# Seven-product sigmoid-gate projections, with sums of the normalised input made early and weight sums made by VectorE

## The reference

```python
h = rmsnorm(x, norm_g)
proj = einsum('bsd,dc->bsc', h, w_in)
a_qkv, z_a, b_qkv, z_b, r_a, r_b = split(proj, ...)   # r_a, r_b: 1024 columns each
y_a = einsum('bsc,cd->bsd', attn_a * silu(z_a), w_pa)  # K = 256
y_b = einsum('bsc,cd->bsd', attn_b * silu(z_b), w_pb)  # K = 512
merged = sigmoid(r_a + b_merge[:1024]) * y_a + sigmoid(r_b + b_merge[1024:]) * y_b
out = rmsnorm(x + einsum('bsd,de->bse', merged, w_out), final_g)
```

## Time and profile before

| | us |
|---|---|
| median of 3 runs | 443.84 (443.66 to 444.29) |
| the profiled execution, its time | 443.48 |
| the profiled execution, its span | 441.7 |
| PE busy | 431.6 |
| DVE, ACT, POOL busy | 212.8, 198.5, 176.3 |

### The profile page before, as it was taken

The page is one execution under the profiler, slowest core; times in us unless marked ns, Lnnn a source line. Parts: engine busy times, 40 slices in busy tenths (PEclk is TensorE's granted clock), DMA queues, the critical chain, the costliest instruction groups (busy, mean ns, idle before and its releaser), DMA issues.

```text
span 441.7 us, 6258 instructions
## 1 busy us (share of the span) xinstructions
PE 431.6 (98%) x2377; PEld 374.5 (85%) x2377; DVE 212.8 (48%) x367; ACT 198.5 (45%) x401; POOL 176.3 (40%) x113
## 2 busy tenths in 40 slices
PE   7899999999999999999999999999999999999995
PEld 6789998899889988988888888888888888888885
DVE  3831244344435446757857664827025173083334
ACT  5743555335544464567555554533223543332111
POOL 4744442243243333646499543534355354200000
PEclk9999999999999999999999999999999999999999
DMA  8962234622452263024122022222222284210421
GB/s 284 286 192 96 96 96 83 159 96 95 91 150 97 96 168 110 25 96 143 49 95 96 0 73 96 96 72 96 95 71 96 95 261 156 113 66 0 149 90 47
DMA packets 40044, 48.31 MB, mean 109 GB/s; under 512 B 3768, under 2 KB 35536, under 8 KB 40016
## 3 DMA queue, kind: packets, MB, share of 16 engines
q1 hardware_dynamic: 37568, 47.72, 34.4%
q10 hardware_dynamic: 2448, 0.21, 0.4%
HBM read 39.48 MB, written 2.15 MB: 94 GB/s over the span
## 4 chain that ended last, share of the span: by engine, by line
PE 96%; DMA 2%; DVE 1%; ACT 1%; SPq 0%; issue 0%; DVEq 0%; ACTq 0%
PE ps L766 20%; PE ps L770 20%; PE ps L767 20%; PE ps L816 4%; PE ps L818 4%; PE ps L817 4%; PE ps L890 3%; PE ps L974 3%; PE ps L975 3%; PE ps L973 3%; PE ps L873 3%; PE ps L917 3%; PE ps L907 2%; DMA xs<-in_x 2%; PE ps L865 1%; PE ps L850 0%
## 5 line engine op out<-in xcount | busy, mean ns | idle before, releaser
L662 POOL TENSOR_TENSOR w_lo<-raw,w_hi 128x1024 fp32r<-128x1024 f32 (+1 forms) x59 | 138.1, 2342 | 175.4 <-ACT w_hi L990 175.4
L766 PE MATMUL ps<-hT_hi,w_hi 128*128 128x512 f32 x336 | 135.0, 402 | 1.1 <-DVE hT_lo L1241 1.1
L770 PE MATMUL ps<-hT_lo,w_hi 128*128 128x512 f32 x336 | 131.2, 390 | 0.0
L767 PE MATMUL ps<-hT_hi,w_lo 128*128 128x512 f32 x336 | 131.1, 390 | 0.0
L770 PEld LDWEIGHTS ps<-hT_lo,w_hi 128*128 128x128 f32 x336 | 63.1, 188 | 13.5
L766 PEld LDWEIGHTS ps<-hT_hi,w_hi 128*128 128x128 f32 x336 | 63.2, 188 | 11.2 <-issue 1.3
L767 PEld LDWEIGHTS ps<-hT_hi,w_lo 128*128 128x128 f32 x336 | 63.3, 188 | 9.9
L990 ACT CAST w_hi<-raw 128x1024 fp32r<-128x1024 f32 (+1 forms) x58 | 59.2, 1020 | 8.3 <-PE ps L770 5.4
L816 PE MATMUL ps<-w_hi,hT_hi 128*128 128x256 f32 x160 | 45.6, 285 | 0.0
L818 PE MATMUL ps<-w_lo,hT_hi 128*128 128x256 f32 x160 | 44.7, 279 | 0.0
L817 PE MATMUL ps<-w_hi,hT_lo 128*128 128x256 f32 x160 | 44.6, 279 | 0.0
(11 more groups left out here) (148 smaller groups left out, 665.6 us busy)
## 6 DMA issues: line engine op xcount, KB each, us to landing
raw<-in_w_in SPq DMA_DIRECT2D x25, 1024.0 KB, 4.9
KTs<-KTs SPq DMA_DIRECT2D x20, 256.0 KB, 3.4
raw<-in_w_out SPq DMA_DIRECT2D x4, 1024.0 KB, 4.8
xs<-in_x SPq DMA_DIRECT2D x4, 512.0 KB, 5.3
raw<-in_w_pb SPq DMA_DIRECT2D x4, 512.0 KB, 4.1
res<-in_x SPq DMA_DIRECT2D x4, 512.0 KB, 3.9
out<-weighted SPq DMA_DIRECT2D x8, 256.0 KB, 2.1
raw<-in_w_in SPq DMA_DIRECT2D x2, 512.0 KB, 8.9
```

What stands on the lines that cost most here:

```text
L662: nc.gpsimd.tensor_tensor(ring(w_lo, n, kt), src, ring(w_hi, n, kt).bitcast(F32), ALU.subtract).then_inc(lo_ready, 1)
L766: pe.matmul(out, wh, hh, start=(k == 0), stop=False)
L767: pe.matmul(out, wl, hh, start=False, stop=False)
L770: return pe.matmul(out, wh, hl, start=False, stop=(k == kts - 1))
```

## The change

The first chunk of `ra` and `rb` (256 columns each) stays as it was. The other six pairs (branch b, chunk c) are computed as a product of matrices cut in two by two: K into 2 x 512, columns into 2 x 128, positions into 2 x 256. With seven products in the place of eight (Winograd's form of Strassen's method) this takes 7 products of 4 blocks of K by 3 matmuls of 256 positions, 84 matmuls, where the two steps had 48 matmuls of 512.

It needs sums of the quarters of the input and of the weights, and sums of the products:

- Four sums of input quarters (`fold`, 10 additions of 128 x 1024 on DVE in steps 2 to 5, all between SBUF tiles), rounded by ACT (`fold_high`), their low parts by DVE (`fold_low`), stored to DRAM (4 x 1 MB) and loaded again (`load_fold`) when the attention has left their place.
- For each of the six parts q: four sums of weight quarters on DVE into two PSUM banks (`sum_begin`, `sum_third`, `sum_last`; the first has both inputs in SBUF), seven roundings by ACT, four low parts by DVE (`sum_low`) and three by POOL (`split_low`).
- Seven products, 256 columns each, in four PSUM banks, put together by `combine` on DVE (7 additions of 256 columns) after a copy of the first by ACT; then the tanh in SBUF by ACT (`squash`).

The tail is now a list of 58 operations (`OPS`): y0 r0 y1 r1 ... y5 r5 y6 y7, a y being two operations of 9 matmuls and an r seven of 12. Weights are prepared six operations ahead (`AHEAD`) in eight slots. `merge` keeps its sum in PSUM. The low parts of `w_out` move from DVE to POOL; its rows 2 to 7 are rounded after the last product (`R_DONE`). `OUT_BANKS` and the output stage stay as they were.

The diff, cut to its core:

```diff
 ND = D // P
-for j in range(ND // 2):
-    CHUNKS += [("ra", C_RA + 256 * j), ("rb", C_RB + 256 * j), ("y", 256 * j)]
+CHUNKS += [("ra", C_RA), ("rb", C_RB)]
...
-OUT_AT = len(CHUNKS) - 3
-LOADS = [("w", c) for c in range(OUT_AT)] + [("out", 0), ("out", 1)] + \
-        [("w", c) for c in range(OUT_AT, len(CHUNKS))] + [("out", 2), ("out", 3)]
...
+SEVEN = [(b, c) for c in range(1, ND // 2) for b in range(2)]
+NSEV = len(SEVEN)
+PARTS = [part for q in range(NSEV) for part in (("y", q), ("r", q))] + [("y", d) for d in range(NSEV, ND)]
+OPS = []
+for kind, c in PARTS:
+    OPS += [(kind, c, p) for p in range(7 if kind == "r" else 2)]
+OP_OF = {op: o for o, op in enumerate(OPS)}
+R_DONE = OP_OF[("r", NSEV - 1, 6)] + 1
+NSLOT = 8
+AHEAD = 6
+LOADS = [("w", c) for c in range(len(CHUNKS))]
+for part in PARTS:
+    LOADS += [("out", 0)] if part == ("y", NSEV - 1) else []
+    LOADS += [part]
+LOADS += [("out", c) for c in (1, 2, 3)]
...
+VLOWS = [item for item in SPLITS if item[0] == "r" and item[2] in (1, 2, 3, 5)]
...
+DUE = {}
+for m in reversed(range(len(SPLITS))):
+    item = SPLITS[m]
+    if item[0] != "wo":
+        DUE[item] = OP_OF[item] - AHEAD + (item[0] == "r" and item[2] == 3)
+    elif item[1] < 2:
+        DUE[item] = DUE[SPLITS[m + 1]]
+    else:
+        DUE[item] = R_DONE + (item[1] - 2) // 2
...
+FOLD_SLOTS = range(2, 7)
+DUMP_AT = 7
...
+        def lows_wait(eng, count):
+            by_vector = sum(1 for item in SPLITS[:max(count - NS, 0)] if item in VLOWS)
+            eng.wait_ge(lo_ready, count - by_vector)
+            if by_vector:
+                eng.wait_ge(lo_by_vector, by_vector)
...
+        def op_source(op):
+            kind, c, p = op
+            if kind == "r":
+                return (quarter(c, 0, 0), sum_bank(1), sum_bank(0), sum_bank(0), quarter(c, 1, 0), sum_bank(1),
+                        quarter(c, 1, 1))[p]
+            t = raw[:, LOAD_OF[("y", c)] % NRAW, 0:6 * P].rearrange("p (k c) -> p k c", k=6)
+            return t[:, 3 * p:3 * p + 3, :]
...
+        def slot_free_wait(eng, o):
+            if o < NSLOT:
+                eng.wait_ge(projected, NS - 3 + o // 2)
+            else:
+                eng.wait_ge(consumed, o - NSLOT + 1)
...
+        def product_out(q, p):
+            return ps[:, PRODUCT_BANKS[(7 * q + p) % 4], 0:256]
...
+                if DUMP_AT <= n < DUMP_AT + 4:
+                    store_fold(n - DUMP_AT)
+                if n == len(CHUNKS) - 1:
+                    sp.wait_ge(folds_out, 64)
+                    sp.wait_ge(scored, _s)
+                    for m in (1, 0, 2):
+                        load_fold(m)
...
             sp.wait_ge(masked, _s)
             sp.dma_start(fg[:, :], final_g.partition_broadcast(P)).then_inc(fg_in, 16)
-            sp.wait_ge(projected, NS - 2)
+            sp.wait_ge(consumed, R_DONE)
...
+            def split_low(item):
+                pool.wait_ge(hi_ready, split_count(item))
+                if item[0] == "wo":
+                    k = item[1]
+                    nc.gpsimd.tensor_tensor(wo("lo", k), raw_out(k), wo("hi", k).bitcast(F32),
+                                            ALU.subtract).then_inc(lo_ready, 1)
+                    return
+                o = OP_OF[item]
+                slot_free_wait(pool, o)
+                nc.gpsimd.tensor_tensor(slot_of(w_lo, o), op_source(item), slot_of(w_hi, o).bitcast(F32),
+                                        ALU.subtract).then_inc(lo_ready, 1)
...
+            for item in SPLITS:
+                if item not in VLOWS:
+                    split_low(item)
...
+            def split_wait(item):
+                pe.wait_ge(hi_ready, split_count(item))
+                lows_wait(pe, split_count(item))
+            def product(o):
+                _, q, p = OPS[o]
+                out = product_out(q, p)
+                split_wait(OPS[o])
+                g = 7 * q + p
...
+                else:
+                    pe.wait_ge(taken[(g - 4) % 7], (g - 4) // 7 + 1)
...
+                wh, wl = slot_of(w_hi, o), slot_of(w_lo, o)
+                for k in range(4):
+                    pe.matmul(out, wh[:, k, :], hh[:, k, :], start=(k == 0), stop=False)
+                    pe.matmul(out, wh[:, k, :], hl[:, k, :], start=False, stop=False)
+                    last = pe.matmul(out, wl[:, k, :], hh[:, k, :], start=False, stop=(k == 3))
+                last.then_inc(consumed, 1)
...
+            def branches(o):
+                _, d, half = OPS[o]
+                split_wait(OPS[o])
+                if half == 0:
...
+                    else:
+                        pe.wait_ge(mrg_lo_ready, d)
+                    if d == ND - 1:
+                        lows_wait(pe, split_count(("r", NSEV - 1, 6)))
...
+            def split_high(item):
+                s, count = raw_waits(("out", item[1] // 2) if item[0] == "wo" else
+                                     item[:2])
                 act.wait_ge(s, count)
-                if k == 0:
-                    act.wait_ge(gated_lo, 6)
-                    act.wait_ge(gated_hi, 6)
-                if k == 5:
-                    act.wait_ge(projected, NS - 2)
-                nc.scalar.copy(wo("hi", k), raw_out(k)).then_inc(wo_hi_ready, 1)
+                if item[0] == "wo":
+                    k = item[1]
+                    if k < 2:
+                        act.wait_ge(gated_lo, 6)
+                        act.wait_ge(valued, NH)
+                    else:
+                        act.wait_ge(consumed, R_DONE)
+                    nc.scalar.copy(wo("hi", k), raw_out(k)).then_inc(hi_ready, 1)
+                    return
+                if item[0] == "r" and item[2] in SUM_AT:
+                    act.wait_ge(sum_ready, 4 * item[1] + SUM_AT[item[2]])
+                o = OP_OF[item]
+                slot_free_wait(act, o)
+                nc.scalar.copy(slot_of(w_hi, o), op_source(item)).then_inc(hi_ready, 1)
+            def fold_high(n):
+                act.wait_ge(folded_full[n], 2 if n % 2 else 3)
...
+            def merged_high(d):
                 act.wait_ge(merged, d + 1)
-                nc.scalar.copy(mrg_hi[:, d, :], ysum[:, d % 2, :]).then_inc(mrg_hi_ready, 1)
+                nc.scalar.copy(merged_part("hi", d), ps[:, ybank(d), :]).then_inc(mrg_hi_ready, 1)
+            def squash(q, j):
+                b, c = SEVEN[q]
+                act.wait_ge(c12_ready if j else c21_ready, q + 1)
+                nc.scalar.activation(gate(b, c, j), gate(b, c, j), ACT.Tanh, scale=0.5,
+                                     bias=hbias[:, 8 * b + 2 * c + j:8 * b + 2 * c + j + 1]).then_inc(gate_ready, 1)
...
+            def take_product(o):
+                _, q, p = OPS[o]
+                if p == 0:
+                    act.wait_ge(consumed, o + 1)
...
+                    nc.scalar.copy(first_copy[:, :], product_out(q, 0)).then_inc(first_copied, 1)
...
+                if s - 1 in FOLD_SLOTS[:4]:
+                    fold_high(s - 1 - FOLD_SLOTS[0])
                 if s >= NS - 2:
-                    for k in (4, 5) if s == NS - 2 else (6, 7):
-                        wo_highs(k)
+                    for o in range(4 * (s - NS), 4 * (s - NS) + 4):
+                        prepare(o)
...
-            merged_high(NS - 1)
+            take_step(NS - 1)
+            for o in range(len(OPS) + 3):
+                prepare(o)
+                if o and o - 1 < len(OPS) and OPS[o - 1][0] == "r":
+                    take_product(o - 1)
+                if o > 1 and o - 2 < len(OPS) and OPS[o - 2][0] == "r" and OPS[o - 2][2] in (5, 6):
+                    squash(OPS[o - 2][1], OPS[o - 2][2] - 5)
+                if o > 2 and OPS[o - 3][0] == "y" and OPS[o - 3][2] == 1:
+                    merged_high(OPS[o - 3][1])
...
+            def merge(d):
+                c, j = d // 2, d % 2
+                ga, gb_ = (gate(b, c, j) for b in range(2))
+                dve.wait_ge(consumed, OP_OF[("y", d, 1)] + 1)
+                if c == 0:
+                    proj_taken_wait(dve, NR0 + j)
+                    proj_taken_wait(dve, NR0 + 2 + j)
+                else:
+                    dve.wait_ge(gate_ready, 4 * c)
+                y = ps[:, ybank(d), :]
+                link(nc.vector.scalar_tensor_tensor(out=y, in0=ga, scalar=1.0, in1=y, op0=ALU.add, op1=ALU.mult))
+                link(nc.vector.scalar_tensor_tensor(out=gb_, in0=gb_, scalar=1.0, in1=ps[:, ybank(d) + 1, :],
...
+                nc.vector.tensor_tensor(y, y, gb_, ALU.add).then_inc(merged, 1)
+            def merged_low(d):
                 dve.wait_ge(mrg_hi_ready, d + 1)
-                nc.vector.tensor_tensor(mrg_lo[:, d, :], acc, mrg_hi[:, d, :].bitcast(F32),
+                nc.vector.tensor_tensor(merged_part("lo", d), ps[:, ybank(d), :], merged_part("hi", d).bitcast(F32),
                                         ALU.subtract).then_inc(mrg_lo_ready, 1)
...
+            def sum_begin(q):
+                one, two = sum_bank(0), sum_bank(1)
```

(102 more changed lines are left out.)

287 lines of the change are left out of this document (179 added, 108 removed).

## The result

The changed kernel takes 452.82 us (median of 4 runs, 450.09 to 453.46) against 443.75 us (443.39 to 444.29) for the kernel before on the same chip: a ratio of 1.0192, interval 1.0147 to 1.0236. It is 9.1 us slower. The prediction said 450.0, slower with 0.80, and a range of 442.5 to 454; the time lies in the range, and just above the forecast's own range of 447.5 to 452. Of the four executions the longer ones had the lower mean granted clock: 450.09 us at 0.992, 452.25 at 0.985, 453.40 at 0.982 and 453.46 at 0.981.

The account below looks back on a forecast made before the run. PE bounds the kernel, busy 431.6 of 441.7 us. Span 441.7 - 4.8 (products) + 3.7 (front) + 2.5 (r5) + 5.0 (y7) = 448.1, or 450.2 on the median's footing, stated as 450; range 442.5 to 454.

Parts of the forecast that it names:

- The products: Matmuls of six pairs of steps: 504 of 256 columns at 0.120 us replace 288 of 512, gain 4.8 us, at most 6.5.
- The front: Early steps: input sums on DVE, alternating with POOL, delay PE at head 0's mask and the exponentials; cost 3.7 us, range 0 to 5.
- The first part: Early steps: head 0's mask stands behind DVE's last input addition, so PE stalls 2.7 us before the scores of head 1.
- The second part: Early steps: ACT rounds sum 3 and loads its table before the third exponential, ready at 61.0 where PE asks at 60.1.
- Rival A: Early steps: DVE and POOL overlap, so the front costs nothing; 446.5 us, chance 0.15.
- The load of r5: Round 4: r5 loads late, DVE stands at its first sum, PE waits before product 6; 2.5 us, from 0 to 3.5.
- Between y6 and y7: Tail: PE waits for merge 6's low part, held back by ACT's w_out roundings and tanh; 5.0 us, 3.8 with ACT free.
- the likeliest case: Whole kernel: all three stalls occur and the clock keeps its level; 450 us, own range 447.5 to 452, chance 0.37.
- rival D: At y7: the clock falls in the stall and PE returns at half clock, 0 to 4.1 us more; 452 us, chance 0.20.
- B: Tail: only the wait between y6 and y7 is left, r5's load being in time; 444.0 or 442.4 us, chance 0.12.
- C: Whole kernel: all stalls are covered, y7's too, and the whole gain arrives; 439.0 or 437.3 us, chance 0.08.
- E: In the order of the rounds: more waits than were found; over 454 us, chance 0.08.

Follow-up runs that it names:

- the three corrections: Changed kernel with y7 waiting only for merge 5, r5 loaded before w_out, and the fourth input sum in step 10: 439.3 us, repeated 438.7 us.
- the first profile and 2.7 in the second: Profiles of the changed kernel: its first measurement, 452.82 us, and its rerun without an edit beside the kernel before, 452.15 us, ratio 1.0187.
- the gap that was filled: Changed kernel with 22 unused matmuls of 512 columns on PE between y6 and the wait of y7: 449.57 us, ratio 1.0132.

## Why the prediction was right, and where it was off

**The products** were sized right: 0.120 us apart, 4.8 us gained, first in the timeline of the changed kernel and then, alone, in the kernel with the three corrections. The choice of the price of the output's rows over that of the value steps decided 1.7 us.

**The front** was right in place and mechanism, and too dear: 3.7 predicted, 1.8 measured. The first part, PE waiting for the mask behind the last addition, was put at 2.7 and is 1.26. Counted from step 0, the last addition ends at 40.9 us and not at the 42.5 of the order I wrote out; so the chain in which DVE and POOL alternate is 1.6 us shorter than laid out. The second part, ACT's rounding and table ahead of the exponentials, was put at 1.0 and is 0.5: the third exponential ends at 60.61, which is 44.7 us from step 0 and not 46.4, 1.7 sooner, and PE's own work before it, the shorter wait counted in, came 1.4 sooner. With three sums early and one late the front costs nothing, so the place of the fourth sum is the cause.

**Rival A** (DVE and POOL overlap) is out: three additions that started while POOL was subtracting lasted 3.3 to 3.4 us, all others of their shape 1.2. What was too dear was the order in which I laid them out.

**Transfers of the sums**: 0 predicted, and none of PE's waits is for one.

**Rounds 0 to 3**: 0 predicted, 14.16 to 14.18 us each. Right.

**The load of r5**: right in each link (the load late, DVE standing at the first sum, the additions behind it, product 6), 2.5 predicted for the wait and 2.1 measured. The step left out is what follows: 1.8 us at half clock. Loading r5 first removed both, 3.8 together.

**Between y6 and y7**: 5.0 predicted, 5.3 measured, by the chain that was written down (ACT with four roundings and two tanh, merge 6, rounding, low part). Taking the wait out and, separately, freeing ACT showed it. The term left out of the forecast is again the clock behind it, 2.4 us in the first profile and 2.7 in the second.

**The clock** is where the likeliest case failed. It was held as rival D with a chance of 0.20, at one place, for 0 to 4.1 us. It came at two places, 1.8 and 2.4 us, and in every profile that had the wait. The rows at hand showed a clock of 0.50 behind the end of PE's work; I treated that as a chance beside the forecast where it belonged in the sum. With the terms as measured the sum is -4.8 + 1.8 + 2.1 + 1.8 + 5.3 + 2.4 = +8.6 us, against +9.1 by the medians and +9.9 by the two profiled executions, of which 1.35 are the start.
The Trainium skill, in "TensorE: Matmul & The Clock Gate", section "Part 1: The HAM clock gate", lets the clock halve when PE is idle; the windows agree (0.50 from 394 us on, in an idle stretch that began at about 390.7), and so does the gap that was filled, with a clock of 1.00. Behind the wait of r4 the clock fell only after PE had gone on.

That the forecast (450.0) came within 2.8 us of the time is partly a matter of two errors with opposite signs: 1.9 too much for the front, 4.2 too little for the clock.

**Rivals B, C and E.** B and C left stalls out, and each of the three was there. C's time, 439.0, is what the kernel reaches when the three are removed (439.3 and 438.7). E, further waits in the rounds, did not occur.

## What to carry to other kernels

Work that saves time on the bounding engine is worth its saving only if no step of its preparation comes late: 4.8 us of matmuls were saved here, and three waits of 1 to 5 us and the slow matmuls behind two of them took 13.4 back. When a wait of the bounding engine is predicted, price the wait and the slow matmuls behind it as one term; here 5.3 brought 2.4 with it, and 2.1 brought 1.8. A wait condition that is written for all members of a loop deserves a look at its last member: one index in it was worth 7.9 us.

## What the runs showed of the hardware that was not expected

- Behind PE's pause of 2.1 us in r4 the clock fell, and it fell after the pause: the matmuls at 369.21 to 370.0 were still 0.12 us apart, those from 370.17 on 0.21. All seven profiles that have this pause show it, with the fall 0.15 to 1.5 us after PE had gone on. In the gap before y7 of the changed kernel it fell while PE was idle, at about 393.9 us, and came back in the window from 400 to 401 (0.63), some 5 us after PE had started again.
- Over the profiles the granted clock in the first stage (12 to 14 us) was 1.00 in some and 0.50 in others, also of the same kernel, and step 0 started between 14.06 and 16.11 us. A single profile can't tell an edit of 1 us from that; distances between starts inside the program can.
- A DVE instruction with both inputs in SBUF stretched from 1.22 to 3.36 us (128 x 1024) and from 0.69 to 1.67 (128 x 512) beside POOL, while the same sum with one input in PSUM kept 0.68 to 0.69 in all six cases. Where DVE had started first, it was POOL that stretched: its subtraction at 52.54, in the middle of an addition that kept its 1.22 us, took 3.21 us in the place of 2.40.
